# Another order of transfers for one block's weight quarters, and its first sum at an earlier place of GpSimd's program

## The reference

```python
# first block
h = h + attention_and_retention(rms_norm(h, attn_norm_w)) @ w_out
m = rms_norm(h, ffn_norm_w)
h = h + (silu(m @ w_gate) * (m @ w_up)) @ w_down        # feed-forward 1, D_FF = 2816
# second block
a = rmsnorm(h, g_mix_2); proj = a @ w_in_2              # the mix
... attention, spatial gating, memory attention ...
f = rmsnorm(h, g_ffn_2)
h = h + (silu(gt) * up) @ w_down_2                      # feed-forward 2; gt, up from f @ w_gate_up_2
```

## Time and profile before

| | |
|---|---|
| median of three runs | 2663.57 us |
| the profiled execution's own time | 2663.69 us |
| its span, first to last instruction | 2661.9 us |
| PE busy in the span | 2630.7 us (99%) |
| DVE, POOL, ACT busy | 1777.1, 1584.5, 1110.7 us |
| mean granted TensorE clock | 0.998 |

### The profile page before, as it was taken

The page is one execution under the profiler, slowest core; times in us unless marked ns, Lnnn a source line. Parts: engine busy times, 40 slices in busy tenths (PEclk is TensorE's granted clock), DMA queues, the critical chain, the costliest instruction groups (busy, mean ns, idle before and its releaser), DMA issues.

```text
span 2661.9 us, 36644 instructions
## 1 busy us (share of the span) xinstructions
PE 2630.7 (99%) x13442; PEld 2145.0 (81%) x13442; DVE 1777.1 (67%) x2505; ACT 1110.7 (42%) x2152; POOL 1584.5 (60%) x1167
## 2 busy tenths in 40 slices
PE   8999999999999999999999999999999999999998
PEld 6777787878888888878888888888887788888887
DVE  7776775687777777781132447773469877777777
ACT  6644432344444434454443335211445444434443
POOL 3232243478888878667732233557325888878884
PEclk9999999999999999999999999999999999999999
DMA  3111102111121211133211011342101111211112
GB/s 141 33 32 33 45 21 93 55 60 59 57 64 60 64 60 57 55 131 111 85 48 47 25 41 56 134 166 72 64 33 43 58 59 60 72 56 56 60 52 84
DMA packets 110924, 172.98 MB, mean 65 GB/s; under 512 B 7968, under 2 KB 61728, under 8 KB 108576
## 3 DMA queue, kind: packets, MB, share of 16 engines
q1 hardware_dynamic: 100416, 133.20, 15.7%
q10 hardware_dynamic: 10336, 37.49, 3.7%
HBM read 154.93 MB, written 15.73 MB: 64 GB/s over the span
## 4 chain that ended last, share of the span: by engine, by line
PE 93%; DVE 3%; POOL 1%; issue 1%; ACT 1%; DMA 0%; SPq 0%; DVEq 0%; ACTq 0%; POOLq 0%
PE PS L1573 14%; PE PS L1575 14%; PE PS L1574 14%; PE PS L1232 10%; PE PS L1234 9%; PE PS L1233 9%; PE PS L1865 2%; PE PS L1866 2%; PE PS L1867 2%; PE PS L1268 1%; PE PS L1271 1%; PE PS L1269 1%; PE PS L1341 1%; PE PS L1607 1%; PE PS L1367 1%
## 5 line engine op out<-in xcount | busy, mean ns | idle before, releaser
L940 POOL TENSOR_TENSOR WH<-WRAW,CST 128x512 fp32r<-128x512 f32 x150 | 170.9, 1139 | 611.5 <-PE PS L1234 541.3
L1232 PE MATMUL PS<-XH,WH 128*128 128x512 f32 x960 | 395.0, 411 | 0.4 <-DVE XL L3812 0.4
L3509 DVE TENSOR_TENSOR H<-H,PS 128x512 f32<-128x512 f32 x560 | 366.4, 683 | 41.9 <-PE PS L1575 41.8
L1234 PE MATMUL PS<-XH,WL 128*128 128x512 f32 x960 | 376.2, 392 | 0.0
L1233 PE MATMUL PS<-XL,WH 128*128 128x512 f32 x960 | 375.5, 391 | 0.0
L986 POOL TENSOR_TENSOR WL<-WRAW,WH 128x512 fp32r<-128x512 f32 x174 | 260.1, 1496 | 91.1 <-ACT WH L2378 78.0
L986 POOL TENSOR_TENSOR WL<-XX,WH 128x512 fp32r<-128x512 f32 x148 | 197.4, 1335 | 101.9 <-ACT WH L2378 101.5
L1573 PE MATMUL PS<-XH,WH 128*128 128x512 f32 x640 | 249.8, 390 | 1.8 <-ACT ACC L2496 1.4
L1574 PE MATMUL PS<-XL,WH 128*128 128x512 f32 x640 | 249.4, 390 | 0.0
L1575 PE MATMUL PS<-XH,WL 128*128 128x512 f32 x640 | 249.4, 390 | 0.0
L1574 PE MATMUL PS<-PL,WH 128*128 128x512 f32 x624 | 243.2, 390 | 0.0
(11 more groups left out here) (456 smaller groups left out, 6087.7 us busy)
## 6 DMA issues: line engine op xcount, KB each, us to landing
WRAW<-ws SPq DMA_DIRECT2D x84, 512.0 KB, 3.4
WRAW<-ws SPq DMA_DIRECT2D x148, 256.0 KB, 2.6
XX<-ws SPq DMA_DIRECT2D x108, 256.0 KB, 2.7
RAWX<-ws SPq DMA_DIRECT2D x68, 256.0 KB, 2.6
gate_spill<-TG ACTq DMA_DIRECT2D x28, 256.0 KB, 2.1
H<-xT ACTq DMA_DIRECT2D x2, 2048.0 KB, 9.6
h_spill<-H ACTq DMA_DIRECT2D x1, 4096.0 KB, 12.9
THB<-gate_spill ACTq DMA_DIRECT2D x4, 1024.0 KB, 5.3
```

The costliest lines, as they stand in the source:

```text
L940: pool.tensor_tensor(WH[:, j, c], WRAW[:, j, c], ONES[:, 0:1].to_broadcast((P, 512)), ALU.mult).then_inc(hi_split, 1)
L1232: pe.matmul(out, WH[:, j, w], rh(kt), start=(n == 0), stop=False)
L1234: last = pe.matmul(out, WL[:, j, w], rh(kt), start=False, stop=(n == len(kts) - 1))
L3509: dve.tensor_tensor(x, x, PS[:, 4 + t], ALU.add).then_inc(h_added, 1)
```

## The change

The quarters of block 2 (the first with seven products), in both feed-forwards and in the mix, are transferred in the order A22, A21, A11, A12 instead of A11, A21, A22, A12. So A22 takes the ring buffer that A11 had, and A11 that of A22. S1 of block 2 moves from the start of block 2 into block 0, behind the second of POOL's low parts of the inputs (n = 7); in the feed-forward it waits for the column sums there instead of for low parts and the gate. In the mix S1 of block 3 moves from behind the low part of P3 of block 2 to behind that of P4.

```diff
+def piece_order(b):
+    return ("A22", "A21", "A11", "A12") if b == 2 else QUARTERS
...
-MIX_PIECE_OF = [("plain" if b < 2 else "fast", b, q) for b in range(MIX_BLOCKS) for q in QUARTERS]
+MIX_PIECE_OF = [("plain" if b < 2 else "fast", b, q) for b in range(MIX_BLOCKS) for q in piece_order(b)]
...
-PIECE_OF = [("plain" if b < 2 else "fast", b, q) for b in range(FT) for q in QUARTERS]
+PIECE_OF = [("plain" if b < 2 else "fast", b, q) for b in range(FT) for q in piece_order(b)]
...
                         pool.tensor_tensor(xl, scaled_input(n % 8, n // 8), xh.bitcast(F32), ALU.subtract).then_inc(x_low2, 1)
+                        if n == 7:
+                            first_sum(f, 2)
...
-                pool.wait_ge(w_low, W_LOW_AT[f] + (SLOT["fast", b - 1, "P5"] + 1 if b > 2 else 8))
+                if b > 2:
+                    pool.wait_ge(w_low, W_LOW_AT[f] + SLOT["fast", b - 1, "P5"] + 1)
+                else:
+                    pool.wait_ge(col_sum, 4 + 6 * f)
...
                     pool.wait_ge(gate_mul, 44 * f + 1)
-                    first_sum(f, b)
                     third_sum(f, b)
...
                 if b == 2 and name == "P1":
-                    mix_first_sum(b)
                     mix_third_sum(b)
...
-                if name == "P3" and b + 1 < MIX_BLOCKS:
+                if name == "P3" and 2 < b < MIX_BLOCKS - 1 or name == "P4" and b == 2:
                     mix_first_sum(b + 1)
...
+                        if n == 7:
+                            mix_first_sum(2)
```

## The result

The changed kernel takes 2676.82 us (median of 5 runs, 2674.11 to 2678.49), the kernel before 2663.57 us beside it (2662.53 to 2668.43). The ratio is 1.0045, with a 95% interval of 1.0035 to 1.0056: 13 us slower, where the forecast was +4.1 us and the range ended at 2672.5. A later set on one chip gave 2673.58 against 2664.16, a ratio of 1.0028 (1.0017 to 1.0039). A time this far above the one before had a chance of 0.38 in the forecast; the size lies outside the range.

What follows compares the result with a forecast made beforehand. The prediction took PE to bound the kernel, others acting only through its waits. Feed-forward 1 +1.6, feed-forward 2 +0.5 and the mix +2.0 summed to +4.1 on 2663.69, so 2667.8 us, range 2664.0 to 2672.5.

Steps and rivals of the forecast that it cites:

- What bounds the kernel: Whole kernel: PE is busy 99% of the span, so other engines' edits move the time only through PE's waits.
- S1 early in the feed-forwards costs nothing: Block 2 of the feed-forwards: POOL's idle time hides the moved S1; 0, with bounds of -1.7 and +1.7.
- The main term of feed-forward 1: S1 of block 3 waits for A22, 3.6 us late, 2.0 won back: +1.6; PE waits before down P1, its 0.87 goes.
- The nine operations: Feed-forward 1, POOL from S1 of block 3 to down P6's low part: 14.4 us before, about 13.2 forecast.
- DVE's price: Feed-forward 1: 2.8 us that DVE working beside POOL adds to the nine operations; 1.2 of it taken as coming back.
- Feed-forward 2: S1 of block 3 starts 2.5 us late for A22, whose landing takes 3.1; 2.0 back, so +0.5.
- The mix: S1 of block 2 waits for A21, PE stands about 2.7 us at n = 9; with block 3's S1, +2.0 together.
- the 1.57 before P6: Mix, block 2: PE's idle time for DVE's input sums, forecast to go by absorbing part of the new wait.
- the second wait, before P1 of block 3: Mix: S1 of block 3 waits for A22, so PE waits 0.9 us more before P1.
- the one on the clock: New waits of 2.5 to 3.3 us: a clock fall can't be excluded, but the sum counts none.
- the rival that priced a fall: The clock falls in one of the new waits: 3.0 us more, 2670.8 us; chance 0.12.
- Given back: Feed-forwards: POOL regains 2.0 us of S1's lateness, 1.2 from DVE running ahead and 0.82 of idle time.

Runs made afterwards that it cites:

- the fifth: Changed kernel with the new order of transfers, but S1 of block 2 back where it stood before the change; 2672.50 us, ratio 1.0024.
- the sixth kernel: Changed kernel with extra matmuls: 11 before down P1, 14 in the mix and 6 near 1860 us; 2667.46 us, ratio 1.0009.
- third: Changed kernel with 7 extra matmuls before down P1 in each feed-forward and 9 in the mix's wait; 2670.56 us, ratio 1.0019.
- eighth kernel: The changed kernel run once more, nothing altered, on one chip beside others; 2673.58 us.
- the first two kernels: Kernel before with the change in the feed-forwards only, 2670.79 us, ratio 1.0021; with it in the mix only, 2667.62 us, ratio 1.0008.

## Why the prediction was wrong

*What bounds the kernel* was right: PE, and only through waits. *S1 early in the feed-forwards costs nothing* was right: it began at 505.23 us, where POOL then waited for ACT again. It even gained a little: PE's wait for DVE's TR near 549 us is 0.31 us in every traced kernel with the early S1 and 0.69 in every one without it, the fifth with the new order among them.

*The main term of feed-forward 1* had the right cause and nearly the right size: A22 landed 3.4 us after its issue and not 4.2, S1 came at 558.41 and not 559.1, PE's new wait was 3.13 us ("some 2.5 to 3.3"), the 0.87 went, and the waits grew by 1.3 (1.6 forecast). The nine operations took 12.8 us (13.2 forecast), so more of DVE's price came back than the 1.2 taken, but the 0.82 us before down P6's low part, which the sum gave back whole, stayed. *Feed-forward 2* was mis-sized by little: +1.3 instead of +0.5, since there too the landing decided, 3.7 us after its issue and not 3.1.

*The mix* was right in its sum of waits: PE waited 3.58 us and not 2.7, the 1.57 before P6 went, +2.0 as forecast, though the second wait, before P1 of block 3, did not come: S1 of block 3 was held for 2.70 us by its transfer, but PE was later still. The 2.0 is met by luck: the first wait was 0.9 us longer than forecast, and the second, forecast at 0.9, is missing.

**The step that failed** is the one on the clock: "The sum goes without it", and the rival that priced a fall "in one of the waits" at 3.0 us with a chance of 0.12. The forecast had one row without a fall (1.57 us) and nothing between that and the end of the kernel; it set three waits of 2.5 to 3.3 us on the side of the 1.57. They were on the other side, all three in both traces of the changed kernel, and each cost 1.0 to 2.2 us beyond its length. The price was read from a row at the kernel's start whose clock column shows 1.00, yet it was near that of one long stretch (2.9 us near 1870 us). The rival counted one fall where three waits of about one length gave occasion for three: at its price +3 x 3.0, 2677, and the range should have reached that. That 2677 is also the measured median is luck: the three falls cost 5.2 together, and 4.3 came from the stretches near 1870 us and at the end, which no term or rival had. Nor do all executions have all of them: those without a trace go down to 2671.4 us at a mean clock of 0.996.

The Trainium skill, "TensorE: Matmul & The Clock Gate", section "HAM oscillation — how this bites in real kernels", says just this: PE idle for long behind a DMA begins its next work at half the clock. These traces agree: behind all 11 waits of 3.1 to 3.6 us in the five traces that have them the clock fell, behind those of 1.2 to 1.6 us around the change it did not, and behind the one of 2.35 us it did.

*Given back:* POOL's operations behind S1 ran faster while DVE had gone ahead, as forecast. PE's short waits of before (0.24 and 0.34) went with the new wait and not with the clock: they are gone in the sixth kernel too, where the clock stayed at 1.00.

What stays open: why the clock falls near 1860 us in some executions and not in others. It fell there in all three traces of the whole change without feeding at this place (changed, third and eighth kernel) and in none of the other five without it. PE's longest waits there are nearly the same before (0.48 and 0.63 us) and after (0.48 and 0.56), so the length of a single wait does not decide it; near 2645 us, in the first two kernels, it fell behind a wait of 0.9 us. With PE fed near 1860 us no traced execution has a fall there, but why it is a matter of chance was not tried.

## What to carry to other kernels

Where PE is the bound, a new wait has two prices: its length, and above some length a stretch at half the clock behind it. Look in the trace for the longest wait that the clock has survived, and price any longer one with the fall as the likelier case, in every place that has it. A short wait is no safeguard either: near 1860 and 2645 us the clock fell behind waits of 0.9 us and less. Moving work earlier on one engine's list moves that list's waits earlier too: look up when each input of the moved instruction lands, and what stands behind it. And a wait that can't be removed may be filled: some forty useless matmuls, 0.23 us each, won back 6 us here.

## What was not expected of the hardware

The run times of an unchanged kernel of 2664 us reach up by 5 us, and the clock goes with them: of 33 runs 21 lie below 2664.4 us, all but one at a mean granted clock of 0.998, and the nine above 2667 us at 0.996 or 0.997. In the 27 runs beside the sixth kernel some lie between, from 2664.9 to 2665.9. With six matmuls of 0.23 us more, in places where PE waits anyway, none of 11 runs lay above 2666.4 us.
